# Mirrored partition halves for the second head kind in the chunk steps of an RWKV-7 layer

## The reference

```python
def step(S, inp):
    r_t, w_t, k_t, v_t, a_t, b_t = inp
    sa = jnp.einsum('bhvk,bhk->bhv', S, a_t)
    S = (S * w_t[:, :, None, :] + sa[..., None] * b_t[:, :, None, :]
         + v_t[..., None] * k_t[:, :, None, :])
    return S, jnp.einsum('bhvk,bhk->bhv', S, r_t)

_, y = lax.scan(step, jnp.zeros((B, H, N, N), jnp.float32), xs)
```

## Time and profile before

| | |
|---|---|
| median of three runs | 1835.14 us |
| the profiled execution | 1840.28 us, span 1838.2 us |
| TensorE busy | 1718.2 us, 93% of the span |
| VectorE / ScalarE / GpSimd busy | 1036.0 / 800.7 / 632.0 us |
| chunk steps of layer 0 | 252.56 to 299.49 us |
| chunk steps of layer 1 | 844.29 to 889.45 us |

### The profile page before, as it was taken

One profiled execution on the slowest core, in us unless ns is written; L12 is line 12 of the kernel. 1 busy time (PEld: TensorE's weight loads), 2 busy tenths in 40 slices (PEclk: granted clock), 3 DMA queues, 4 the chain that ended last, 5 costly groups with the idle time before them and its releaser, 6 DMA issues. The chain is left out here.

```text
span 1838.2 us, 26011 instructions
## 1 busy us (share of the span) xinstructions
PE 1718.2 (93%) x10688; PEld 1373.8 (75%) x10688; DVE 1036.0 (56%) x1367; ACT 800.7 (44%) x1200; POOL 632.0 (34%) x344
## 2 busy tenths in 40 slices
PE   8999989999999899899999999989999999987783
PEld 6877778888888787688888888868888986544441
DVE  4346744666665325584556766443116627866675
ACT  2455522333223335542333222344337736866673
POOL 1336612424444434751243444433421021322210
PEclk7999989999999899998999999989999999999997
DMA  8223321215444323322122544333420067999994
GB/s 344 81 92 106 90 77 36 92 58 192 171 166 171 126 92 96 96 85 77 54 85 66 209 175 169 138 126 126 149 92 1 1 240 265 382 388 395 389 392 178
DMA packets 82605, 287.97 MB, mean 157 GB/s; under 512 B 30473, under 2 KB 30601, under 8 KB 65332
## 3 DMA queue, kind: packets, MB, share of 16 engines
q1 hardware_dynamic: 76708, 275.87, 41.6%
q0 software_dynamic: 5040, 8.25, 1.4%
q10 hardware_dynamic: 736, 2.14, 0.3%
HBM read 274.50 MB, written 22.61 MB: 162 GB/s over the span
## 5 line engine op out<-in xcount | busy, mean ns | idle before, releaser
L1525 POOL TENSOR_TENSOR wmem_r<-wmem,wmem_r 128x1024 fp32r<-128x1024 f32 x170 | 420.2, 2473 | 696.4 <-ACT wmem_r L1041 685.5
L721 PE MATMUL banks<-h_hi_r,wmem_r 128*128 128x512 f32 x1632 | 511.2, 392 | 6.9 <-POOL wmem_r L1525 6.9
L721 PEld LDWEIGHTS banks<-h_hi_r,wmem_r 128*128 128x128 f32 x1632 | 307.9, 189 | 77.0 <-POOL wmem_r L1525 9.4
L1041 ACT ACTIVATE wmem_r<-wmem 128x1024 fp32r<-128x1024 f32 x170 | 180.2, 1060 | 405.2 <-DMA wmem<-wstream 402.2
L721 PE MATMUL banks<-hT_r,wmem_r 128*128 128x512 f32 x816 | 319.0, 391 | 0.0
L721 PEld LDWEIGHTS banks<-hT_r,wmem_r 128*128 128x128 f32 x816 | 154.0, 189 | 31.3
L2725 DVE TENSOR_TENSOR slots_r<-slots,wmem_r 128x1024 fp32r<-128x1024 f32 x102 | 121.9, 1217 | 57.7 <-ACT wmem_r L2418 52.1
L2806 POOL TENSOR_TENSOR wmem_r<-wmem,wmem_r 128x1024 fp32r<-128x1024 f32 x30 | 74.8, 2493 | 202.3 <-ACT wmem_r L2276 202.3
L992 PE MATMUL banks<-slots_r,wmem_r 128*128 128x512 f32 x512 | 127.7, 389 | 0.0
L1465 DVE SCALAR_TENSOR_TENSOR ztp<-xT,c_act,ztp 128x256 f32<-128x256 f32 x168 | 122.8, 731 | 6.0
L741 PE MATMUL banks<-wmem_r,h_hi_r 128*128 128x512 f32 x384 | 118.9, 391 | 0.0
(11 more groups left out here) (450 smaller groups left out, 3043.1 us busy)
## 6 DMA issues: line engine op xcount, KB each, us to landing
wmem<-wstream SPq DMA_DIRECT2D x206, 512.0 KB, 3.3
slots<-experts SPq DMA_DIRECT2D x80, 1024.0 KB, 24.5
xT<-ada SPq DMA_DIRECT2D x24, 1024.0 KB, 5.8
xT<-experts SPq DMA_DIRECT2D x16, 1024.0 KB, 25.0
slots<-ada SPq DMA_DIRECT2D x8, 1024.0 KB, 18.0
x_keep<-xT SPq DMA_DIRECT2D x2, 2048.0 KB, 17.4
xT<-x_keep SPq DMA_DIRECT2D x2, 2048.0 KB, 8.1
dil_rows<-dil_once SPq DMA_DIRECT2D x1, 2560.0 KB
```

What stands on the lines that cost most here:

```text
L721: mm = nc.tensor.matmul(o, r(lhs[:, k, :]), r(rhs[:, k, :]), start=(k == 0 and i == 0), stop=(k == KD - 1 and i == 2))
L1041: inc(nc.scalar.activation(r(chunk(b)[0]), w, ACT.Copy), "w_high")
L1525: inc(g.tensor_tensor(r(lo), lo, r(hi), ALU.subtract), "w_split")
```

## The change

Head e = 1 now uses the other partition half: `v_side` and `u_side` take `e`. The matmuls of the value part, correction and output part alternate between e = 0 and e = 1, and so between two column halves. The token-row transposes become 64x64 matmuls against the identity (`token_rows`). The copy of `w{m}1` goes from ScalarE to VectorE, that of `u{m}1` from VectorE to ScalarE. Both masks of a gram now follow the multiply that raises `s_ready`, and in the ring of banks the `u` banks are opened ahead of the grams.

```diff
-        v_side = lambda m: side_of[m % 2]
-        u_side = lambda m: side_of[(m + 1) % 2]
-        sub_of = lambda m, q: slice(u_side(m).start + q * SUB, u_side(m).start + (q + 1) * SUB)
+        v_side = lambda m, e: side_of[(m + e) % 2]
+        u_side = lambda m, e: side_of[(m + e + 1) % 2]
+        sub_of = lambda p, q: slice(side_of[1 - p].start + q * SUB, side_of[1 - p].start + (q + 1) * SUB)
         uv_of = lambda m: v_tok[:, m // 2, :] if m % 2 else uv_even[m // 2 % 2]
         bk_of = lambda m: (bk_odd if m % 2 else bk_even)[:, m // 2, :]
         per_head = lambda a: a.rearrange("p (c e f) -> p e c f", c=CW, e=2)
+        by_parity = lambda a: a.rearrange("p n f -> p (n f)").rearrange("p (i e f) -> p e i f", e=2, f=RW_D)
...
-                job(f"w{m}{e}", "w_ready", 1 + 2 * m + e)
+                job(f"w{m}{e}", f"w_ready{e}", 1 + m)
+            for e in range(2):
+                job(f"u{m}{e}", f"u_ready{e}", 1 + m)
             if m + GRAMS_FIRST < STEPS:
                 gram_jobs(m + GRAMS_FIRST)
-            for e in range(2):
-                job(f"u{m}{e}", "u_ready", 1 + 2 * m + e)
...
+        for m in range(STEPS - GRAMS_FIRST):
+            for e in range(2):
+                FULL[f"u{m}{e}"] += 2
+                FULL[f"gram{m + GRAMS_FIRST}{e}"] -= 2
...
+            def token_rows(what, n, z, side):
+
+                o = [open_bank(f"t{what}{n + e}") for e in range(2)]
+                for i in range(2 * CW):
+                    at, c = 2 * (n + i // CW), i % CW
+                    for m in (at, at + 1):
+                        for e in range(2):
+                            half = side_of[e]
+                            mm = nc.tensor.matmul(o[e][side(m, e), i * RW_D:i * RW_D + RW_D], z[half, c, m * STEP:m * STEP + STEP],
+                                                  ident[half, half], start=True, stop=True)
+                            if i == 2 * CW - 1 and m % 2 == 1:
+                                full(mm)
...
-            for n in range(NT):
-                transposes(f"tv{n}", [V_[:, c, n * P:n * P + P] for c in range(CW)])
-            for n in range(NT):
-                o = open_bank(f"tb{n}")
-                for c in range(CW):
-                    for m in (2 * n, 2 * n + 1):
-                        mm = nc.tensor.matmul(o[u_side(m), c * P:c * P + P], A_[:, c, m * STEP:m * STEP + STEP], ident, start=True, stop=True)
-                full(mm)
+            for n in range(0, NT, 2):
+                token_rows("v", n, V_, v_side)
+            for n in range(0, NT, 2):
+                token_rows("b", n, A_, u_side)
             after("bk_ready", 2)
-            for n in range(NT):
-                transposes(f"tk{n}", [K_[:, c, n * P:n * P + P] for c in range(CW)])
+            for n in range(0, NT, 2):
+                token_rows("k", n, K_, v_side)
...
 
                 after("gram_ready", 2 * m + 2)
                 if m % 2 == 0:
-                    after("v_copied", m // 2 + 1)
+                    after("v_copied", m + 2)
                 o_w = [open_bank(f"w{m}{e}") for e in range(2)]
-                for e in range(2):
-                    for c in range(CW):
-                        mm = nc.tensor.matmul(o_w[e][u_side(m), heads[c]], gm[:, m % 4, e, c, 1, :], uv[:, e, c, :],
+                for c in range(CW):
+                    for e in range(2):
+                        mm = nc.tensor.matmul(o_w[e][u_side(m, e), heads[c]], gm[:, m % 4, e, c, 1, :], uv[:, e, c, :],
                                               start=(c == 0), stop=(m == 0 and c == CW - 1), skip_group_check=True)
-                    if m == 0:
-                        full(mm)
+                        if m == 0 and c == CW - 1:
+                            full(mm)
                 if m > 0:
                     after("s_ready", m)
-                    state_part(o_w, KK, m, u_side(m), False, True)
+                    state_part(o_w, KK, m, u_side, False, True)
+                o_u = [open_bank(f"u{m}{e}") for e in range(2)]
                 if m + GRAMS_FIRST < STEPS:
                     gram(m + GRAMS_FIRST)
 
-                for e in range(2):
-                    o_u = open_bank(f"u{m}{e}")
-                    after("w_ready", 2 * m + e + 1)
-                    after("z_ready", 2 * (m // 4) + 2)
-                    for c in range(CW):
-                        mm = nc.tensor.matmul(o_u[u_side(m), heads[c]], zt[u_side(m), RW_H * (m // 2) + 2 * c + e, :],
-                                              w_sb[u_side(m), e * CW * RW_D + c * RW_D:e * CW * RW_D + (c + 1) * RW_D], start=True, stop=True)
-                    full(mm)
+                after("w_ready0", m + 1)
+                after("w_ready1", m + 1)
+                after("z_ready", 2 * (m // 4) + 2)
+                for c in range(CW):
+                    for e in range(2):
+                        mm = nc.tensor.matmul(o_u[e][u_side(m, e), heads[c]], zt[u_side(m, e), RW_H * (m // 2) + 2 * c + e, :],
+                                              w_sb[u_side(m, e), e * CW * RW_D + c * RW_D:e * CW * RW_D + (c + 1) * RW_D], start=True, stop=True)
+                        if c == CW - 1:
+                            full(mm)
 
                 if m < STEPS - 1:
                     o_s = open_bank(f"s{m}")
                 o_y = [open_bank(f"y{m}{e}") for e in range(2)]
                 if m > 0:
-                    state_part(o_y, R_, m, v_side(m), True, False)
-                after("u_ready", 2 * m + 2)
+                    state_part(o_y, R_, m, v_side, True, False)
+                after("u_ready0", m + 1)
+                after("u_ready1", m + 1)
                 if m < STEPS - 1:
                     for c in range(CW):
                         for e in range(2):
                             mm = nc.tensor.matmul(o_s[side_of[e], heads[c]], bk[:, e, c, :], uv[:, e, c, :], start=True, stop=True)
                     full(mm)
-                for e in range(2):
-                    for c in range(CW):
-                        mm = nc.tensor.matmul(o_y[e][v_side(m), heads[c]], gm[:, m % 4, e, c, 0, :], uv[:, e, c, :],
+                for c in range(CW):
+                    for e in range(2):
+                        mm = nc.tensor.matmul(o_y[e][v_side(m, e), heads[c]], gm[:, m % 4, e, c, 0, :], uv[:, e, c, :],
                                               start=(m == 0 and c == 0), stop=(c == CW - 1), skip_group_check=True)
-                    full(mm)
+                        if c == CW - 1:
+                            full(mm)
 
...
-                for e in range(2):
-                    inc(nc.scalar.activation(w_sb[u_side(m), e * CW * RW_D:(e + 1) * CW * RW_D], bank(f"w{m}{e}")[u_side(m), 0:CW * RW_D], ACT.Copy), "w_ready")
+                inc(nc.scalar.activation(w_sb[u_side(m, 0), 0:CW * RW_D], bank(f"w{m}0")[u_side(m, 0), 0:CW * RW_D], ACT.Copy), "w_ready0")
+                o = bank(f"u{m}1")[u_side(m, 1), 0:CW * RW_D].rearrange("p (c f) -> p c f", c=CW)
+                inc(nc.scalar.activation(per_head(uv_of(m)[u_side(m, 1)])[:, 1], o, ACT.Copy), "u_ready1")
                 if m % 2 == 1 and m // 2 < RING:
                     high(FIRST["retq"] + m // 2)
                 for e in range(2):
-                    o = bank(f"y{m}{e}")[v_side(m), 0:CW * RW_D].rearrange("p (c f) -> p c f", c=CW)
-                    inc(nc.scalar.activation(per_head(y_tok[v_side(m), m // 2, :])[:, e], o, ACT.Copy), "y_ready")
+                    o = bank(f"y{m}{e}")[v_side(m, e), 0:CW * RW_D].rearrange("p (c f) -> p c f", c=CW)
+                    inc(nc.scalar.activation(per_head(y_tok[side_of[m % 2], m // 2, :])[:, e], o, ACT.Copy), "y_ready")
...
-                mask = con("odd" if m % 2 else "even").unsqueeze(1).broadcast_to([P, CW, P])
+                mask = con("odd" if (m + e) % 2 else "even").unsqueeze(1).broadcast_to([P, CW, P])
                 inc(v.tensor_tensor(gm[:, m % 4, e].rearrange("p c k t -> p c (k t)"), o, mask, ALU.mult), "gram_ready")
 
             for m in range(GRAMS_FIRST):
                 for e in range(2):
                     gram_mask(m, e)
             for m in range(STEPS):
-                if m + GRAMS_FIRST < STEPS:
-                    gram_mask(m + GRAMS_FIRST, 0)
-                for e in range(2):
-                    o = bank(f"u{m}{e}")[u_side(m), 0:CW * RW_D].rearrange("p (c f) -> p c f", c=CW)
-                    inc(v.tensor_copy(per_head(uv_of(m)[u_side(m)])[:, e], o), "u_ready")
+                inc(v.tensor_copy(w_sb[u_side(m, 1), CW * RW_D:2 * CW * RW_D], bank(f"w{m}1")[u_side(m, 1), 0:CW * RW_D]), "w_ready1")
+                o = bank(f"u{m}0")[u_side(m, 0), 0:CW * RW_D].rearrange("p (c f) -> p c f", c=CW)
+                inc(v.tensor_copy(per_head(uv_of(m)[u_side(m, 0)])[:, 0], o), "u_ready0")
                 if m < STEPS - 1:
                     o = bank(f"s{m}")[:, 0:CW * RW_D].rearrange("p (c f) -> p c f", c=CW)
                     if m == 0:
@@ -1360,7 +1380,8 @@
```

(33 more changed lines are left out.)

## The result

The changed kernel is slower: 1847.98 us in the median of seven runs (1845.66 to 1850.82), the kernel before 1836.03 in as many. The ratio is 1.0067, with a 95% interval of 1.0053 to 1.0080. The forecast was 1832.5 us with a range of 1820 to 1842.

A forecast was written before the change was run, and what follows sets the result against it. TensorE bounds masked steps; without grams it pauses for copies. Step 0 gains 2.0 and 2.9 us, the later steps lose 1.1 a layer: 2.7 gained, 1840.28 to 1837.6, less 5.1 to the median, 1832.5 us; range 1820 to 1842.

The forecast's parts named there:

- The parts on TensorE: Value and output parts of 16 records, alternating between column halves: 0.53 us each, from 1.02 and 0.93.
- Correction to update: From start of correction to start of state update: 1.25 us instead of 1.63, by shorter correction and copies on two engines.
- both waits: Multiply behind GpSimd's subtraction in steps 1, 3, 5, 1.96 us each; TensorE 0.84 us for the second mask, steps 1 to 4.
- GpSimd's lead: In odd steps GpSimd's subtraction starts 0.26 us ahead of VectorE's multiply, above the 0.16 seen in a rotary-part wait.
- step 0: First step of each layer, at the lower clock: 2.9 us less in layer 0, 2.0 less in layer 1.
- the stretches: From step 1's first state part to the projections, per layer: 38.1 us against 37.0 before, 1.1 longer.
- T + 1.68: Step 5, masks before it but no gram: the correction starts 1.68 us after the state part starts (T).
- T + 1.70: The copy of w{m}1, queued on VectorE behind the masks, is ready 1.70 us after the state part starts (T).
- The step that failed: the clock: Rival, 15%: TensorE's clock falls behind odd-step pauses, 1.4 us a fall, six falls 8.4 us, 1840.9 us.
- The port isn't taken: Rival, 18%: odd-step multiply starts ahead of GpSimd and loses nothing; six steps shorter by 1.96 us, 11.8 us, 1820.7 us.
- The grams don't wait: Rival, 13%: second mask or ring earlier than reckoned in steps 1 to 4; 0.55 us less in eight steps, 1828.1 us.
- the column halves don't overlap: Rival, 7%: value part, correction and output get no overlap between column halves; 7.6 us a layer, 1847.7 us.

The follow-up runs named there:

- b1: Kernel before, with the chunk's rounding in steps 1, 3 and 5 held back until the step's first u copy is done; 1845.0 us, ratio 1.0045 to before.
- e3: Changed kernel with the value part of steps 2, 4 and 6 computed five times instead of once; 1842.4 us, ratio 1.0044 to the kernel before.
- e1: Changed kernel with the chunk's rounding in steps 1, 3 and 5 moved behind the copy of w{m}0; 1830.3 us, ratio 0.9967 to the kernel before.
- a2: The changed kernel profiled once more, without an edit, for a second look at the clock; 1851.5 us in one run.
- e2: Changed kernel with the first gram mask put back between the copies of w{m}1 and u{m}0; 1842.8 us, ratio 1.0037 to the kernel before.
- e6: Changed kernel with early rounding and split masks, its three parts issued all e = 0 first, then e = 1; 1830.0 us, ratio 0.9955 to before.

## Why the prediction was wrong

**What held.** The parts on TensorE: 0.47 us where 0.53 was forecast. Correction to update: 1.22 (260.43 to 261.65 in the changed kernel's timeline), forecast 1.25. The place and the reason of both waits: the port taken by GpSimd in exactly the six multiplies named, and grams behind the second mask in steps 1 to 4. The first held narrowly: of the 0.26 us forecast for GpSimd's lead 0.10 were left.

**Right by luck: step 0.** It took 5.80 and 7.53 us instead of 9.94 and 8.18, 4.8 gained where 4.9 were forecast, but 4.1 in layer 0 and 0.65 in layer 1 against the 2.9 and 2.0 of the forecast. How long step 0 takes hangs on when the clock comes back: in layer 0 at 261.6 in the profile before, 0.9 us ahead of the end of step 0. In b1, whose edit leaves step 0 as it was before, it came back at 253.1, and step 0 took

```profile
250.44 1.97 PE L889 MATMUL banks<-rstd,gm_mem 128*64 128x64 f32 x16
...
257.93 0.62 PE L875 MATMUL banks<-state,slots 64*64 64x64 f32 x13
```

7.49 us in layer 0 and 7.64 in layer 1, 3.0 less than in the profile that the forecast was read from. So the same 13.3 us of the changed kernel's two steps 0 are a gain of 4.8 us against the one profile and of 1.8 against the other.

**The sizes in the chain.** With hardly any fall (e3) the stretches are 40.35 and 39.93 us, forecast 38.1. An odd step took 7.4 instead of 7.10, an even one 5.35 instead of 5.14, step 5 7.0 instead of 6.55, step 6 4.4 instead of 4.11, step 7 3.4 instead of 2.98. Two terms were small. GpSimd started 1.09 behind the update, not 0.93 (262.74 - 261.65), because ScalarE's rounding ran a little later. And the way from a state part to the correction was 0.2 to 0.3 us longer in every step: TensorE started 0.25 us behind the end of the second mask (259.28 to 259.53) and of the copy of `w{m}1` (300.46 to 300.71), where the forecast put next to nothing; in step 5 it even put the correction at T + 1.68, ahead of the copy that it needs at T + 1.70. Behind the multiply it was the 0.05 that was forecast (265.37 to 265.42); why the two differ isn't shown. Over two layers that is 4.1 us, and it turns the forecast gain of 2.7 us into a loss of 1.4, still within what counts as no change.

**The step that failed: the clock.** The forecast's sum put it at nothing, and kept it as a rival of 15%, with 1.4 us a fall, 1840.9 us at six falls. It is what happened: four falls in the steps of one profile, five in the other. The argument against it was that the clock stayed full in the kernel before with pauses of 0.51 and 0.23 us. But the forecast had itself worked out pauses of 2.0 and 0.84 us with 0.46 of work between, for every odd step, and a pause like that is near the 2.63 us of the earlier trace rows, behind which the clock fell. It was also priced too low. A fall was charged with the gram and correction of one step; it lasted through the rest of the step or into the next, so update, output and value part were at half rate too: step 4 took 7.73 us against the 5.35 of step 2, 2.4 us. In the profiled execution the falls cost 6.9 us, and filling the pauses (e3) gave 5.6 us by the runs. By e1 the six collisions and the falls that they cause are worth 17.7 us together, 12.1 of it the longer steps.

**The total.** In the profiled execution the steps, step 0 included, are 8.5 us longer than before (50.36 + 50.20 against 46.93 + 45.16); in a2 9.4 us (50.63 + 50.83). The medians differ by 12.0. That execution of the changed kernel is the fastest of its seven (1845.66), that of the kernel before is slower than its median. Some 3 us of the difference are placed in no stretch, and stay open; the 3.0 us by which step 0 differs between the profile before and b1 show that one execution can be off by as much.

**Rivals.** "The port isn't taken" did not happen: a lead of 0.10 us, less than the 0.16 of the earlier trace rows, was enough. Its price was right in kind but short: taking the collision away gives 17.7 us, not 11.8, because the clock comes along. "The grams don't wait" and "the column halves don't overlap" did not happen.

## What to carry to other kernels

When parts on one engine get shorter, the work of two others that used to miss each other can meet: look for every pair of VectorE operations with two SBUF inputs and GpSimd operations near it, and move whichever has slack. Here one chunk's rounding, 1.05 us on an engine with time to spare, placed one copy later, turned a gain of 0.33% (e1) into a loss of 0.67%. Charge a new pause of 2 us on TensorE twice, once for itself and once for the clock behind it: here 12.1 and 5.6 us for six of them.

## What the runs showed of the hardware

- VectorE's multiply with two SBUF inputs waited for all of GpSimd's subtraction at leads of 0.10 us (changed kernel, 2.53 us) and 0.40 us (b1, 2.22 us).
- TensorE's clock fell to 1.2 GHz behind pauses of 2.0 to 2.14 us in the odd steps, nine times of twelve in the two profiles of the changed kernel, and four times of six in e2, where the pause behind the state part is 0.25 instead of 0.84. It didn't fall each time, nor at the same steps. With the 2.14 us filled by repeated matmuls and the 0.84 left (e3) it fell behind none of six. More matmuls took 5.6 us less time.
- Matmuls of 64 columns in different column halves overlap over the border of two groups of instructions: 1.43 us for two parts of 16 records (e6) against 1.95 in one half, and 0.47 for one part alternating between the halves.
